# Seven products in place of eight for the gates of two branches, and copies of flipped attention rows on ScalarE, in one decoder layer

## The chip, the cores and the metric

The kernel runs on one core of a Trainium2 chip. The metric is the device time of one execution in microseconds (us). TensorE (PE in the rows) does matmuls into eight PSUM banks; VectorE (DVE), ScalarE (ACT) and GpSimd (POOL) do the element-wise work; SyncE (SP) starts most DMAs. Every engine runs its own queue strictly in order, and semaphores order the engines against each other.

## The reference, cut to what matters

One layer of a decoder for 512 prompt tokens and 8x8 sample tokens, 576 rows in all, all in float32. Three branches (A a conformer convolution, B an attention over the best-scoring keys, C a gated MLP over chunks) are each projected, gated and added:

```python
h = x * (1 + sc1) + sh1
z = jnp.einsum('btd,de->bte', h, w_in) + b_in
a_glu, q, k, v, qi, ki, wi, uv, gate_logits = jnp.split(z, SPLIT_OFFSETS, axis=-1)
...
g_a, g_b, g_c = jnp.split(jax.nn.sigmoid(gate_logits), 3, axis=-1)
merged = g_a * (y_a @ w_pa) + g_b * (y_b @ w_pb) + g_c * (y_c @ w_pc)
x = layer_norm(ALPHA * x + (1 + g1) * (merged @ w_o), ln1_g, ln1_b)
h2 = x * (1 + sc2) + sh2
x = layer_norm(ALPHA * x + (1 + g2) * moe(h2, ...), ln2_g, ln2_b)
```

A gate is a product of h (1024 wide) with a 1024x1024 part of w_in, a projection one of y (512 wide) with a 512x1024 matrix. The attention picks 128 keys for a prompt row (66 for a sample row) by the scores of an indexer, and `moe` routes each row to two of 16 experts.

## The kernel before

A list of steps, `plan`, is written by hand in `make_plan` and `full_plan`, and every engine's block walks the same list and issues its own part of each step; so the list sets the order of all five queues. Activations lie transposed, features on partitions: `HT` holds h as 8 slices of 128 features by 576 tokens, `YT` the branches' outputs as 4 slices. Tokens are worked in two halves of 288 (`HALF`).

The stage at issue has 48 pairs of a gate and a projection, (branch, tile f of 128 output features, half h), first A, then C, then B. `("gate", x, f, h)` is 8 matmuls of 128x128 weights with 128x288 activations into one bank, `("proj", x, f, h)` 4 such matmuls (L1923 in both, a helper). ScalarE takes a tanh of the gate (L1194) and a copy of the projection (L1201), GpSimd adds one to the tanh, multiplies and adds it to `MG` (L912, L917, L918; the last two pairs go to VectorE, L1742 and L1744). `GT` and `PJ`, the outputs of ScalarE, have two buffers each, and `merged` counts finished pairs.

Between the pairs of A and C stand the steps of the attention, by the table `sides`, in units of 128 prompt rows and two heads: `dots` (indexer scores, L2119; VectorE L1613, L1616, L1618), `tk` (top-k rounds of VectorE, L1345 and L1346), `lg` (logits on TensorE, L2152; softmax on VectorE from L1640 to L1655 with exponents on ScalarE, L1062), `pt` (flips of the probabilities through TensorE, L1927, and a copy of the result from PSUM to `PTT` on VectorE, L1668) and `pv` (product with the values, L2193, copied by VectorE, L1682). A unit's `lg`, `pt` and `pv` stand one pair apart. The units grow: 128, 256, 384 and 512 keys. `("pv", "s")` is the last of them, for the sample rows (L2198 and L2203), and VectorE then prepares rows for the layer norm (`prepare_rows`, L1356 to L1360) from transfers that start behind it.

PSUM banks are used in three rings: three banks for gates and projections (`mm`), two for flips (`tt`), three for attention products (`at`). A step waits for the bank to be freed by whoever read it last. Behind the stage come W_o (L1957), layer norm, the router, which sets `order_known`, and the experts, whose weights SyncE brings in behind that.

## Time and profile before

| | |
|---|---|
| runs of the kernel before | 1064.9, 1067.6, 1067.71 us; median 1067.6 |
| profiled execution | 1068.1 us, of it span 1066.0 |
| mean granted clock of TensorE | 0.971 |
| busy over the span | PE 1006.0 us (94%), DVE 497.1 (47%), POOL 248.7 (23%), ACT 188.0 (18%) |
| gates and projections of A, C, B | about 276 to 406, 406 to 540, 540 to 639 us |
| W_o, layer norm, router | 640 to about 740 us |
| experts | about 740 to 1030 us |

A share of busy time is a mean over stages with different limits, so the rows below are read by stretch. A timeline's row gives start, duration (of a run of instructions that follow each other, with their count), engine, line, and in brackets the idle time ahead of it with what ended it. A float32 matmul leaves two records. A duration that stands behind a count covers the whole run; a mean in ns is that of one instruction and overlaps its neighbours on TensorE.

### The profile page before, as it was taken

What the parts mean: (1) busy time and instruction counts of PE and PEld (TensorE: products, weight loads), DVE (VectorE), ACT (ScalarE), POOL (GpSimd) and SP (SyncE); (2) the same over time, 40 slices, a digit from 0 to 9 for tenths busy, and PEclk for the clock granted to TensorE, in tenths of its full rate; (3) what the DMA queues carried; (4) which work ended last, traced back from release to release, by engine and by line L of the source; (5) the groups of instructions that cost most, each with busy time, mean ns of one, the idle gap of its engine ahead of it and who ended that gap; (6) DMA issues with size and microseconds to landing.
All of it is one profiled execution on the core that took longest, in us unless ns stands there. A gap on an engine that the chain in (4) does not pass through costs nothing. (4 is left out here: it accounts for less than half of the span.)

```text
span 1066.0 us, 23313 instructions
## 1 busy us (share of the span) xinstructions
PE 1006.0 (94%) x9543; PEld 705.4 (66%) x9543; DVE 497.1 (47%) x1295; ACT 188.0 (18%) x444; POOL 248.7 (23%) x284
## 2 busy tenths in 40 slices
PE   4999999999999999999999999986998999999994
PEld 3777777567776767667777774565666666866663
DVE  2122899983467888855114003678322221101146
ACT  2010112213221222221111110011111111111104
POOL 0000002734121213222335420000211212422123
PEclk8998999999999999999999999996999999999997
DMA  9964743654505206114072309134599899999994
GB/s 308 308 131 132 219 159 112 219 188 137 208 13 173 65 17 201 45 32 119 11 180 77 119 1 365 40 137 180 221 420 419 340 409 396 414 393 409 408 251 92
DMA packets 94001, 214.96 MB, mean 202 GB/s; under 512 B 23572, under 2 KB 48407, under 8 KB 89797
## 3 DMA queue, kind: packets, MB, share of 16 engines
q1 hardware_dynamic: 78388, 186.20, 49.0%
q0 software_dynamic: 6672, 19.67, 6.1%
q10 hardware_dynamic: 8841, 7.64, 2.6%
q8 instruction: 77, 1.26, 0.5%
q14 instruction: 23, 0.19, 0.1%
HBM read 201.12 MB, written 16.92 MB: 205 GB/s over the span
## 5 line engine op out<-in xcount | busy, mean ns | idle before, releaser
L1923 PE MATMUL banks<-arena 128*128 128x288 f32 (+7 forms) x1842 | 446.9, 398 | 6.0 <-issue 2.1
L1923 PEld LDWEIGHTS banks<-arena 128*128 128x128 f32 (+2 forms) x1842 | 332.1, 192 | 113.1 <-issue 31.3
L2308 PE MATMUL banks<-arena 128*32 128x256 f32 x3136 | 183.4, 382 | 5.8 <-issue 4.5
L2308 PEld LDWEIGHTS banks<-arena 128*32 128x32 f32 x3136 | 113.0, 109 | 66.7 <-issue 8.2
L1851 DVE TENSOR_TENSOR arena<-arena,banks 128x128 f32<-128x128 f32 x49 | 14.1, 288 | 215.0 <-ACT arena L1240 214.7
L2330 PE MATMUL banks<-arena 128*32 128x256 f32 x1568 | 95.3, 378 | 0.0
L912 POOL TENSOR_SCALAR arena<-arena 128x288 f32<-128x288 f32 x46 | 43.1, 937 | 198.8 <-ACT arena L1194 198.8
L970 POOL DMA_INDIRECT expert_rows<-arena,ints x44 | 42.9, 974 | 190.7 <-ACT arena L1251 190.7
L1317 DVE SCALAR_TENSOR_TENSOR arena<-arena 128x512 f32<-128x512 f32 x120 | 82.0, 744 | 0.0
L1937 PE MATMUL banks<-arena 128*128 128x288 f32 x256 | 69.2, 428 | 2.7 <-DVEq L1335 2.7
L2330 PEld LDWEIGHTS banks<-arena 128*32 128x32 f32 x1568 | 53.5, 109 | 23.2 <-issue 0.4
L1937 PEld LDWEIGHTS banks<-arena 128*128 128x128 f32 x256 | 49.9, 199 | 19.2 <-DVEq L1335 4.3
L1957 PE MATMUL banks<-arena 128*128 128x512 f32 x128 | 56.5, 594 | 1.1 <-DVE arena L1744 1.1
L1927 PE MATMUL banks<-arena 128*128 128x128 f32 (+7 forms) x295 | 45.1, 283 | 12.4 <-DMA arena<-constants 4.9
L1927 PEld LDWEIGHTS banks<-arena 128*128 128x128 f32 (+7 forms) x295 | 33.6, 147 | 25.7 <-issue 13.6
L1194 ACT ACTIVATE arena<-banks,arena 128x288 f32<-128x288 f32 x48 | 24.0, 501 | 132.3 <-PE banks L1923 128.9
L1957 PEld LDWEIGHTS banks<-arena 128*128 128x128 f32 x128 | 23.7, 189 | 29.0 <-issue 29.0
L876 POOL TENSOR_TENSOR arena<-arena 9x512 f32<-9x512 f32 x8 | 13.2, 1652 | 126.0 <-ACTq L1089 126.0
L1240 ACT ACTIVATE arena<-banks 128x128 f32<-128x128 f32 x49 | 13.6, 278 | 161.5 <-PE banks L2308 161.5
L858 POOL TENSOR_TENSOR arena<-arena 128x1 f32<-128x1 f32 (+1 forms) x15 | 8.4, 560 | 118.4 <-DVE arena L1298 118.4
L1251 ACT ACTIVATE arena<-banks,arena 128x256 f32<-128x256 f32 x44 | 20.9, 474 | 76.0 <-PE banks L2330 76.0
L917 POOL TENSOR_TENSOR arena<-arena 128x288 f32<-128x288 f32 x30 | 25.6, 854 | 33.7 <-ACT arena L1201 33.4
(303 smaller groups left out, 938.9 us busy)
## 6 DMA issues: line engine op xcount, KB each, us to landing
arena<-in_w_e_gate SPq DMA_DIRECT2D x16, 2048.0 KB, 13.0
arena<-in_w_e_up SPq DMA_DIRECT2D x16, 2048.0 KB, 14.9
arena<-in_w_e_down SPq DMA_DIRECT2D x16, 2048.0 KB, 21.2
arena<-in_w_ada SPq DMA_DIRECT2D x8, 2048.0 KB, 10.6
arena<-in_w_in SPq DMA_DIRECT2D x8, 2048.0 KB, 9.8
arena<-in_w_ada SPq DMA_DIRECT2D x8, 1024.0 KB, 11.6
arena<-in_x_prompt SPq DMA_DIRECT2D x8, 512.0 KB, 6.4
arena<-in_w_in SPq DMA_DIRECT2D x14, 256.0 KB, 8.2
```

The lines of the kernel that those rows point to most:

```text
L912: own.link(pool.tensor_scalar(GT[:, z, :], GT[:, z, :], 1.0, None, ALU.add))
L917: own.link(pool.tensor_tensor(PJ[:, z, :], GT[:, z, :], PJ[:, z, :], ALU.mult))
L970: pool.indirect_dma_start(quarters, bass.IndirectOffsetOnAxis(ints[:, I_DEST + d:I_DEST + d + 1], 0), YR[:, yr_of(d), :], None).then_inc(s ...
L1194: act.activation(GT[:, n % 2, :], mm.tile(key)[:, 0:HALF], ACT.Tanh, bias=PARH[:, r:r + 1], scale=0.5).then_inc(mm.free(key), 1)
L1251: act.activation(YR[:, yr_of(d), :], banks[6 + d % 2][:, 0:256], ACT.Copy, scale=WBLK[:, d:d + 1]).then_inc(ev("yo_up"), 1)
L1317: stt(ACC[:, j, 0:SEQ], arena[:, bass.ds(w + (A_AE + j * EXT), SEQ)], arena[:, bass.ds(w + (A_CK + j * CW), 1)], ACC[:, j, 0:SEQ], ALU.mul ...
L1923: last = pe.matmul(out, a, b, start=k == 0, stop=k == len(pairs_) - 1)
L1927: return pe.transpose(out, src, ident[0:src.shape[0], 0:src.shape[0]])
L1937: return pe.matmul(early_in(key).tile(key)[:, 0:HALF], a_rows[:, k, a:a + P], HT[:, k, h * HALF:h * HALF + HALF], start=k == 0, stop=k == ...
L1957: last = pe.matmul(ps, MG[:, k, t * P:t * P + P], w[k], start=k == 0, stop=k == KT - 1)
L2308: last = pe.matmul(out, HG[:, g % 2, k, a:a + BLK], both_weights(i, k, c), start=k == 0, stop=k == KT - 1)
L2330: last = pe.matmul(banks[6 + b % 2][BLK * c:BLK * c + BLK, 0:256], HETB[:, b % 2, k, :], w[:, k, 256 * c:256 * c + 256], start=k == 0, sto ...
```

## The change

**Gates.** Eight pairs of tiles, f and f+1 with f = 0, 2, 4, 6 of C and of B (`FAST`), are computed together as a 2x2 block product: the weights in quarters w11, w12, w21, w22 (half of the contraction by tile), the activations in quarters x11, x12, x21, x22 (half of the contraction by half of the tokens). Seven products of four matmuls each, step `("seven", x, m, k)`, take the place of four gates of eight: 1 = w11 x11, 2 = w12 x21, 5 = s1 t1, 6 = s2 t2, 3 = s4 x22, 7 = s3 t3, 4 = w22 t4. The sums s of the weights (step `("sum", "w", m, k)`, four of 128x512 for each pair, the third one written over w21) and t of the activations (`("sum", "t", k)`, four of 128x1152, once) are made by VectorE, L1488 in the kernel after. The results are added up by VectorE too, seven additions of 128x288 a pair, in PSUM or into the buffers `part` and `cross`; ScalarE copies product 1 to `part`, and takes the tanh of a product only when VectorE has added to it (`seven_added`).

**Projections.** For the pairs f = 0, 2, 4 of B (`FIVE`) the projections are made in the same way, `("five", ...)`: seven products of two matmuls, four sums of weights of 128x256 (`"v"`) for each pair, four of activations of 128x576 (`"y"`) once, and seven additions a pair. These products use the `at` ring.

**Order.** The sums of the first pair's weights stand behind the attention steps of pair ("A", 7, 0); the sums of activations stand between products 1 and 2 of the first pair of C; other pairs' weight sums stand in the pair ahead. Within a pair of C the order is 1, 2, attention, 6, projection, 5, attention, 3, projection, 7, attention, projection, 4, projection, attention. `prepare_rows` is split into ten steps that stand in the last two pairs of `FIVE`.

**Flipped rows.** The copies of `pt` for the prompt units go from VectorE (L1668) to ScalarE. The copies for the sample rows stay.

**Others.** A few semaphores are merged (the convolution's weights into `small_in`, and three of the router into `routed_full`), 1024 floats are added to the arena, and the scratch for software DMA is set to 8192.

```diff
+A_SUMS = A_SM + 164
+A_END = A_SUMS + 2 * 512
...
+FAST = [("C", f) for f in (0, 2, 4, 6)] + [("B", f) for f in range(0, KT, 2)]
+FIVE = [m for m, (x, f) in enumerate(FAST) if x == "B" and f < KT - 2]
+SUMS_AFTER = {("A", KT - 1, 0): [("sum", "w", 0, k) for k in range(4)]}
...
-    for x in "AC":
-        for f in range(KT):
-            for h in range(2):
-                plan += [("gate", x, f, h), ("proj", x, f, h)] + sides[n]
-                n += 1
-    plan += [("gate", "B", 0, 0), ("pv", "s"), ("gate", "B", 0, 1), ("proj", "B", 0, 0), ("proj", "B", 0, 1)]
-    for f in range(1, KT):
+    for x, f in [("A", f) for f in range(KT)] + [("C", f) for f in range(FAST[0][1])]:
         for h in range(2):
-            plan += [("gate", "B", f, h), ("proj", "B", f, h)]
+            plan += [("gate", x, f, h)] + ([("sum", "t", 2)] if (x, f, h) == ("C", 3, 1) else [])
+            plan += [("proj", x, f, h)] + sides[n] + SUMS_AFTER.get((x, f, h), [])
+            n += 1
+
+    for m, (x, a) in enumerate(FAST):
+        g = lambda *ks: [("seven", x, m, k) for k in ks]
+        proj = lambda f, h: [("proj", x, a + f, h)]
+        nxt = lambda *ks: [("sum", "w", m + 1, k) for k in ks] if m + 1 < len(FAST) else []
+        rows = lambda *ks: [("rows", "ps"[m - FIVE[1]], k) for k in ks] if m in FIVE[1:] else []
+        side = lambda k: sides[16 + 2 * FAST[0][1] + 4 * m + k] if x == "C" else []
+        if m not in FIVE:
+            late = [("sum", "t", k) for k in range(4)] if (m, FAST[0][1]) == (0, 0) else []
+            plan += g(1) + late + g(2) + side(0) + g(6) + proj(0, 0) + g(5) + side(1) + g(3) + nxt(0) + proj(0, 1) + g(7) + nxt(1, 2)
+            plan += side(2) + proj(1, 1) + g(4) + nxt(3) + proj(1, 0) + side(3)
+            continue
+        q = lambda *ks: [("five", x, m, k) for k in ks]
+        own = lambda *ks: [("sum", "v", m, k) for k in ks]
+        y = lambda k: [("sum", "y", k)]
+        if m == FIVE[0]:
+            plan += g(1) + [("pv", "s")] + g(2) + own(0, 1) + g(6) + y(0) + g(5) + y(1) + q(1, 2) + y(2) + own(2) + g(3) + nxt(0)
+            plan += q(6) + y(3) + own(3) + q(5, 3) + nxt(1) + g(7) + nxt(2) + q(7) + nxt(3) + g(4) + q(4)
+            continue
+        plan += g(1) + q(1) + g(2) + q(2) + own(0, 1) + g(6) + rows(0) + q(6) + own(2) + g(5) + rows(1) + q(5) + own(3) + g(3) + nxt(0) + q(3) + nxt(1)
+        plan += g(7) + nxt(2) + q(7) + rows(2) + nxt(3) + g(4) + rows(3) + q(4) + rows(4)
...
+            elif kind == "seven":
+                _, x, m, k = key
+                if k == 1:
+                    act.wait_ge(*mm.full(key))
+                    if m:
+                        act.wait_ge(*added(m - 1, 4))
+                    act.activation(part, mm.tile(key)[:, 0:HALF], ACT.Copy).then_inc(mm.free(key), 1)
+                elif k in tile_of:
+                    x, f, h = fast_tile(m, k)
+                    n = pair_no[(x, f, h)]
+                    act.wait_ge(*added(m, k))
+                    act.wait_ge(ev("merged"), n - 1)
+                    r = R_G + "ABC".index(x) * KT + f
+                    act.activation(GT[:, n % 2, :], mm.tile(key)[:, 0:HALF], ACT.Tanh, bias=PARH[:, r:r + 1], scale=0.5).then_inc(mm.free(key), 1)
...
+            elif kind == "five" and key[3] == 1:
+                m = key[2]
+                act.wait_ge(*at.full(key))
+                if m > FIVE[0]:
+                    act.wait_ge(*added_y(m - 1, 4))
+                act.activation(part_y, at.tile(key)[:, 0:HALF], ACT.Copy).then_inc(at.free(key), 1)
...
+            elif kind == "pt" and key[1] != "s":
+                _, i, c = key
+                u = unit_no[(i, c)]
+                if u == 0:
+                    act.wait_ge(ev("cv_out"), 16 * 9)
+                else:
+                    act.wait_ge(*at.full(("pv",) + units[u - 1]))
+                k = P * (i + 1)
+                for n in range(NKV):
+                    kk = key + (n,)
+                    act.wait_ge(*tt.full(kk))
+                    act.activation(PTT[:, n, 0:k], tt.tile(kk)[:, 0:k], ACT.Copy).then_inc(tt.free(kk), 1)
...
+        def half_sum(key):
+
+            what, m, k = key[1], key[2], key[-1]
+            if what in "ty":
+                x11, x12, x21, x22 = h_quarters if what == "t" else y_quarters
+                t1, t2, t3, t4 = t_sums if what == "t" else y_sums
+                if k == 0:
+                    dve.wait_ge(*(mm.full(("proj", "A", KT - 1, 1)) if what == "t" else mm.full(("proj", "C", KT - 1, 0))))
+                else:
+                    dve.wait_ge(*summed(what, min(k - 1, 1)))
+                if (what, k) == ("t", 2) and FAST[0][1]:
+                    dve.wait_ge(*mm.full(("gate", "C", 3, 1)))
+                out, a, b, op = ((t1, x12, x11), (t2, x22, t1), (t3, x22, x12), (t4, x21, t2))[k] + (ALU.subtract,)
+            else:
+                w11, w12, w21, w22 = w_quarters(m, 4 if what == "w" else 2)
+                s1, s2, s4 = w_sums if what == "w" else v_sums
+                if k == 0:
+                    x, a = fast_pair(m)
+                    dve.wait_ge(*arrived_at[("g", x, a // 4)])
+                    if what == "w" and m:
+                        dve.wait_ge(*mm.full(fast_key("seven", m - 1, 3)))
+                    if what == "v" and m > FIVE[0]:
+                        dve.wait_ge(*at.full(fast_key("five", m - 1, 3)))
+                else:
+                    dve.wait_ge(*summed(what, m, k - 1))
+                out, a, b, op = ((s1, w21, w22, ALU.add), (s2, s1, w11, ALU.subtract), (s4, w12, s2, ALU.subtract), (w21, w11, w21, ALU.subtract))[k]
+            tt_(out, a, b, op).then_inc(ev("summed"), 1)
...
+        def seven(key, ps):
+
+            _, x, m, k = key
+            ps = ps[:, 0:HALF]
+            if k == 2:
+                dve.wait_ge(*mm.taken(fast_key("seven", m, 1)))
+                tt_(ps, ps, part, ALU.add).then_inc(ev("seven_added"), 1)
+            elif k == 6:
+                dve.wait_ge(*added(m, 2))
+                tt_(part, ps, part, ALU.add).then_inc(ev("seven_added"), 1)
+                dve.wait_ge(*added(m, 6))
+                dve.sem_inc(mm.free(key), 1)
+            elif k == 5:
+                tt_(cross, ps, part, ALU.add).then_inc(ev("seven_added"), 1)
+                dve.wait_ge(*added(m, 5))
+                dve.sem_inc(mm.free(key), 1)
+            elif k == 3:
+                tt_(ps, ps, cross, ALU.add).then_inc(ev("seven_added"), 1)
+            elif k == 7:
+                tt_(part, ps, part, ALU.add).then_inc(ev("seven_added"), 1)
+                dve.wait_ge(ev("seven_added"), 7 * m + 5)
+                tt_(ps, ps, cross, ALU.add).then_inc(ev("seven_added"), 1)
+            elif k == 4:
+                dve.wait_ge(*added(m, 7))
+                tt_(ps, ps, part, ALU.add).then_inc(ev("seven_added"), 1)
...
+            dve.wait_ge(*added_y(m, k))
+            dve.sem_inc(at.free(key), 1)
...
-                if key == ("pv", "s"):
-                    prepare_rows()
...
+            elif kind in ("seven", "five"):
+                _, x, m, k = key
+                n, w_, t_ = (4, "w", "t") if kind == "seven" else (2, "v", "y")
+                if k == 1:
+                    got(("g", x, fast_pair(m)[1] // 4))
+                if key == ("five", "B", FIVE[0], 1):
+                    pe.wait_ge(ev("yb_up"), 17)
+                if k in (5, 6, 3, 7):
+                    pe.wait_ge(*summed(w_, m, {5: 0, 6: 1, 3: 2, 7: 3}[k]))
+                if k in (5, 6, 7, 4):
+                    pe.wait_ge(*summed(t_, {5: 0, 6: 1, 7: 2, 4: 3}[k]))
+                w, x_ = fast_operands(m, n)[k]
+                last = group(ps[:, 0:HALF], [(w[:, j, :], x_[:, j, :]) for j in range(n)])
...
-    nc = bacc.Bacc("TRN2", target_bir_lowering=False, num_devices=1)
+    nc = bacc.Bacc("TRN2", target_bir_lowering=False, num_devices=1, dynamic_dma_scratch_size=8192)
```

The queue of VectorE around the start of C, before: the top-k rounds end, then the copy of `pv` (L1682), the copies of `pt` (L1668) and the softmax (L1640 to L1655).

```order
L1345 MAX arena<-arena 128x8
L1346 MATCH_REPLACE arena<-arena 128x512
L1682 COPY arena<-banks 128x128
L1668 COPY arena<-banks 128x384 x2
L1640 SCALAR_TENSOR_TENSOR arena<-banks,arena 128x384
L1649 ISA arena<-arena 128x384
L1649 ISA arena 128x1
L1651 TENSOR_SCALAR arena<-arena 128x1
```

The same queue now, from the end of the rounds in the last step of A: L1488 are the sums of activations, L1496 the addition to product 2, L1880 the copy of `pv`, L1850 the softmax's first instruction.

```order
L1457 MAX arena<-arena 128x8
L1458 MATCH_REPLACE arena<-arena 128x512
L1488 TENSOR_TENSOR arena<-arena 128x1152 x2
L1488 TENSOR_TENSOR arena<-arena 128x4x288
L1488 TENSOR_TENSOR arena<-arena 128x1152
L1496 TENSOR_TENSOR banks<-banks,arena 128x288
L1880 COPY arena<-banks 128x128
L1850 SCALAR_TENSOR_TENSOR arena<-banks,arena 128x384
```

The four sums and an addition now stand between the rounds and the copy of `pv`, and the copies of `pt` are gone. A little further on, behind that softmax, stand the additions to products 6 (L1499) and 5 (L1503), behind three top-k rounds:

```order
L1864 RECIPROCAL arena<-arena 128x1
L1865 TENSOR_SCALAR arena<-arena 128x384
L1457 MAX arena<-arena 128x8
L1458 MATCH_REPLACE arena<-arena 128x512
L1457 MAX arena<-arena 128x8
L1458 MATCH_REPLACE arena<-arena 128x512
L1457 MAX arena<-arena 128x8
L1458 MATCH_REPLACE arena<-arena 128x512
L1499 TENSOR_TENSOR arena<-banks,arena 128x288
L1503 TENSOR_TENSOR arena<-banks,arena 128x288
L1880 COPY arena<-banks 128x128
```

So a bank that product 6 holds is freed only when VectorE has gone through the rounds. TensorE's queue at the start of C before, from the logits (L2152) at the end of A through one gate and its projection to the attention steps that follow (L2193 `pv`, L1927 `pt`):

```order
L2152 MATMUL banks<-arena 128x384 [waits at_free1]
L2152 MATMUL banks<-arena 128x384 [waits at_free2]
L1923 MATMUL banks<-arena 128x288 [waits slot_in3,mm_free2]
L1923 MATMUL banks<-arena 128x288 x7
L1923 MATMUL banks<-arena 128x288 [waits slot_in3,mm_free0]
L1923 MATMUL banks<-arena 128x288 x3
L2193 MATMUL banks<-arena 64x128 [waits t_free0,t_free1,at_free0]
L2193 MATMUL banks<-arena 64x128 x5
```

And now, from the logits of the first attention step within the pair on: product 6, a projection, product 5, the next attention step and product 3 (all products and projections are L2119).

```order
L2350 MATMUL banks<-arena 128x384 [waits at_free2]
L2119 MATMUL banks<-arena 128x288 [waits summed,mm_free2]
L2119 MATMUL banks<-arena 128x288 x3
L2119 MATMUL banks<-arena 128x288 [waits yct_up,slot_in3,mm_free0]
L2119 MATMUL banks<-arena 128x288 x3
L2119 MATMUL banks<-arena 128x288 [waits summed,mm_free1]
L2119 MATMUL banks<-arena 128x288 x3
L2391 MATMUL banks<-arena 64x128 [waits t_free0,t_free1,at_free0]
L2391 MATMUL banks<-arena 64x128 x5
L2123 MATMUL banks<-arena 128x128 [waits probs_ready,t_free1]
```

Gates of eight matmuls that waited for weights and a bank have become products of four, and three of each seven products wait for VectorE's sums (`summed`).

## Rows read from the trace of the kernel before

**Rows 1.** Busy time by stretch: PE, PEld, DVE, ACT, POOL, granted clock, DMA share, GB/s
```profile
380.00:400.00 20.00, 19.24 (x69) 12.33 (x68) 15.71 (x40) 4.92 (x13) 3.49 (x5) 0.91 0.10 26
400.00:420.00 20.00, 19.44 (x111) 13.96 (x110) 16.93 (x46) 5.80 (x14) 6.70 (x13) 1.00 0.68 225
420.00:440.00 20.00, 20.00 (x134) 14.12 (x133) 18.41 (x40) 3.15 (x8) 7.57 (x9) 1.00 0.16 47
...
600.00:620.00 20.00, 20.00 (x84) 15.53 (x83) 0.00 (x0) 3.23 (x7) 7.89 (x10) 1.00 0.09 33
```

**Rows 2.** TensorE's waits, 280 to 660: us in total, times, longest
```profile
PE banks L2152 <- DVE arena L1682: 1.2, 1, 1.2
PE banks L1957 <- DVE arena L1744: 1.1, 1, 1.1
```

**Rows 3.** Timeline of TensorE in A: start, us, then the run
```profile
332.70 0.70 PE L2152 MATMUL banks<-arena 64*128 64x256 f32 x2 [1.22 <-DVE arena L1682]
333.94 0.70 PE L2152 MATMUL banks<-arena 64*128 64x256 f32 x2 [0.54 <-DVE arena L1613]
334.56 7.78 PE L1923 MATMUL banks<-arena 128*128 128x288 f32 x24
...
385.17 1.07 PE L2152 MATMUL banks<-arena 64*128 64x384 f32 x2 [0.60 <-DVE arena L1616]
386.18 7.57 PE L1923 MATMUL banks<-arena 128*128 128x288 f32 x24
```

**Rows 4.** Timeline of TensorE in C and B
```profile
406.43 6.09 PE L1923 MATMUL banks<-arena 128*128 128x288 f32 x24
412.46 0.88 PE L2193 MATMUL banks<-arena 128*64 128x128 f32 x12
...
414.92 6.10 PE L1923 MATMUL banks<-arena 128*128 128x288 f32 x24
...
435.23 1.13 PE L2152 MATMUL banks<-arena 64*128 64x512 f32 x4
...
438.28 6.10 PE L1923 MATMUL banks<-arena 128*128 128x288 f32 x24
...
592.01 46.86 PE L1923 MATMUL banks<-arena 128*128 128x288 f32 x192 [0.30 <-PE banks L1923]
```

**Rows 5.** Timeline of VectorE around the start of C and at the rows' preparation
```profile
403.45 0.68 DVE L1346 MATCH_REPLACE8 arena<-arena 128x512 f32<-128x512 f32 x1
...
406.63 0.56 DVE L1640 SCALAR_TENSOR_TENSOR arena<-banks,arena 128x384 f32<-128x384 f32 x1
...
410.87 0.69 DVE L1345 MAX8 arena<-arena 128x8 f32<-128x512 f32 x1
...
415.42 0.29 DVE L1682 COPY arena<-banks 128x128 f32<-128x128 f32 x1
...
571.75 0.69 DVE L1356 TENSOR_SCALAR arena<-arena 128x1024 f32<-128x1024 f32 x1 [21.92 <-DMA arena<-in_ln_b]
...
575.59 1.82 DVE L1360 TENSOR_TENSOR arena<-arena 128x1024 f32<-128x1024 f32 x1
...
581.75 1.81 DVE L1360 TENSOR_TENSOR arena<-arena 64x1024 f32<-64x1024 f32 x1
```

**Rows 6.** VectorE's groups by line and shape, 280 to 660: busy us, mean ns
```profile
L1668 DVE COPY arena<-banks 128x512 f32<-128x512 f32 x8 | 5.2, 686 | 1.7 <-PE banks L1927 1.7
L1618 DVE TENSOR_TENSOR arena<-arena 128x512 f32<-128x512 f32 x3 | 2.1, 693 | 0.1
L1359 DVE TENSOR_TENSOR arena<-arena 128x1024 f32<-128x1024 f32 x1 | 1.2, 1225 | 0.0
L1742 DVE SCALAR_TENSOR_TENSOR arena<-arena,banks 128x288 f32<-128x288 f32 x2 | 0.9, 454 | 54.4 <-PE banks L1923 54.4
```

**Rows 7.** Busy time by stretch, the experts (columns as in rows 1)
```profile
740.00:1030.00 290.00, 285.04 (x5193) 190.21 (x5189) 63.04 (x179) 41.64 (x105) 68.29 (x71) 0.99 0.93 371
```

**Rows 8.** Timeline of GpSimd in B
```profile
576.41 1.66 POOL L918 TENSOR_TENSOR arena<-arena 128x288 f32<-128x288 f32 x1
...
587.35 0.79 POOL L918 TENSOR_TENSOR arena<-arena 128x288 f32<-128x288 f32 x1
```

More of the change, by code:

```diff
@@ L527, in build_in, with fast_tile @@
     pos = {k: n for n, k in enumerate(plan)}
-    pairs = [(x, f, h) for x in "ACB" for f in range(KT) for h in range(2)]
+    tile_of = {2: (0, 0), 3: (0, 1), 7: (1, 1), 4: (1, 0)}
+    def fast_tile(m, k):
+        x, a = fast_pair(m)
+        return x, a + tile_of[k][0], tile_of[k][1]
+    pairs = [k[1:] if k[0] == "proj" else fast_tile(k[2], k[3]) for k in plan if k[0] == "proj" or k[0] == "five" and k[3] in tile_of]
     pair_no = {k: n for n, k in enumerate(pairs)}
@@ L904, in _ @@
                 rstd(rows_of(key[1]))
-            elif kind == "proj":
-                _, x, f, h = key
+            elif kind == "proj" or kind == "five" and key[3] in tile_of:
+                x, f, h = key[1:] if kind == "proj" else fast_tile(key[2], key[3])
                 n = pair_no[(x, f, h)]
@@ L910, in _ @@
                     continue
-                pool.wait_ge(*mm.taken(("gate", x, f, h)))
+                pool.wait_ge(*gate_up(x, f, h))
                 own.link(pool.tensor_scalar(GT[:, z, :], GT[:, z, :], 1.0, None, ALU.add))
-                pool.wait_ge(*mm.taken(key))
+                pool.wait_ge(*(mm.taken(key) if kind == "proj" else added_y(key[2], key[3])))
                 if x == "A":
@@ L1486, in _ @@
                 continue
+            if kind == "sum":
+                half_sum(key)
+                continue
+            if kind == "rows":
+                prepare_rows(*key[1:])
+                continue
             ring_of = {"M": mm, "T": tt, "A": at}[ring_name(key)]
-            mine = kind in ("par", "ck", "ws", "st", "cT", "mT", "xTs", "bd", "lnA1", "mix", "dots", "wo", "cum", "near")
+            mine = kind in ("seven", "five") and key[3] > 1 or kind in ("par", "ck", "ws", "st", "cT", "mT", "xTs", "bd", "lnA1", "mix", "dots", "wo", "cum", "near")
             if mine:
@@ L1564, in _ @@
                     conv()
+            elif kind == "seven" and key[3] > 1:
+                seven(key, ps)
+            elif kind == "five" and key[3] > 1:
+                five(key, ps)
             elif kind == "lnA1":
@@ L1979, in _ @@
                 continue
+            if kind in ("sum", "rows"):
+                continue
             ring_of = {"M": mm, "T": tt, "A": at}[ring_name(key)]
@@ L2154, in _ @@
                 else:
[L2155 removed]
+                    pe.wait_ge(ev("masked_up"), 2 + c + 1)
                     if c == 0:
```

135 lines of the change are left out of this document (97 added, 38 removed), and 2 rows, old and new, of the table kinds.

## The prediction

> **What bounds the kernel now.** I read four views in this order. The busy time by stretch [rows 1] shows TensorE at 19 to 20 of every 20 us from the gates of A to the end of the gates of B: this stage is bound by matmuls. It also shows what else is full: VectorE is busy 16.93 and 18.41 us of 20 in 400 to 440, where branch C begins, and has nothing to do in 600 to 620. TensorE's waits between 280 and 660 [rows 2] are few; the longest are 1.2 us before logits in A and 1.1 before W_o. The timeline of TensorE [rows 3] shows what the waits in A cost beyond themselves: after 1.22 and 0.54 us the next gate and projection (24 records) took 7.78 us, after 0.60 us they took 7.57, against 6.09 elsewhere [rows 4]. The granted clock of the stretch with the second is 0.91, that of its neighbours 1.00 [rows 1]: part of it ran at the lower level (1.2 of 2.4 GHz). So such a wait costs its length and some 1.5 to 1.7 us behind it. Last, what follows this stage: from 740 to 1030 the DMA share is 0.93 at 371 GB/s [rows 7]. These are expert weights, whose transfers from the third expert on wait for the routing, and the routing for W_o. A microsecond gained before W_o starts that stage a microsecond earlier and isn't taken back by it; I count it in full.
>
> **Matmuls saved.** A gate is 8 and a projection 4 matmuls of 128x288, two records each. In C 24 records start 6.03 us apart (406.43 to 412.46, [rows 4]): 0.5025 us for one matmul, 4.02 for a gate, 2.01 for a projection or one of the seven products. In B 192 records take 46.86 us [rows 4], 0.488 for a matmul. Eight pairs go from 32 to 28 matmuls and three pairs of projections from 16 to 14: 16 fewer in C, 8.0 us, and 22 fewer in B, 10.7 us. Nothing hides matmuls in this stage, so all 18.7 us lie on the path, if what the new products wait for is ready.
>
> **Flipped rows to ScalarE.** VectorE loses 32 copies of up to 0.686 us [rows 6]. ScalarE is busy 3 to 6 us of 20 here [rows 1]; TensorE issues the product that such a copy waits for ahead of its flips, so I see no new wait there. In A this takes VectorE time away right ahead of the waits on logits, 1.22 + 0.54 + 0.60 = 2.4 us. A little may remain, and a few waits on the copies themselves go as well. I take 2.4; the bounds are 0 (the logits wait for something else) and 2.9.
>
> **The first pair of C: the new waits.** This decides the result. I walk VectorE's queue with durations of before, in the clock of before (both engines come some 2.4 us earlier, which moves both alike). VectorE ends the top-k rounds ahead of C at 404.13 [rows 5]. Now come four sums of weights, 128x512; such a sum takes 0.693 [rows 6], 0.72 with the gap: 2.9. Then the copy of an attention product, 0.5 with its semaphore, a unit's softmax, 406.63 to 410.87, 4.24, and three top-k rounds, 410.87 to 415.42, 4.55 [rows 5]: 416.3. Only then stand the sums of the activations, 128x1152. From 0.693 at 512 and 1.225 at 1024 [rows 6] the slope gives 1.36; one sum at 1024 took 1.82 [rows 5], which would make 2.0. I take 1.4, since the 1.82 goes with GpSimd at work (rival 2) and GpSimd has no gate to work on at this point. The second of them is ready at 419.1.
> - Product 6 needs it. TensorE starts C at 406.43, does two products (4.02) and the attention step (412.46 to 414.92, 2.46 [rows 4]) and stands at 412.9: **6.2 us of waiting**.
> - Product 3 needs the bank of product 6, so VectorE's addition of product 6. In the queue before it stand two more sums (2.8), an addition, a copy (0.5), a softmax (4.24) and three rounds (4.55). An addition of 128x288 I price by the nearest row, 0.454 [rows 6], 0.5 with the gap and up to 0.65 where it waits for itself. From 419.1 that makes 432.2. TensorE needs three times 2.01, then 0.9 for one attention product, 426.1, waits for the softmax's rows at 427.1 (**1.0 us**), does 0.9 of flips, and from 428.0 waits for the bank: **4.3 us**.
> - In the second pair the flips of the first 512-wide unit wait for its softmax. From 431.7 VectorE has six additions (3.2), two copies (1.0), seven rounds with their end (11.0), four sums (2.9) and this softmax (4.24 grows by its width to some 5.0): 454.8. TensorE has from 432.3 eight groups of 2.01 and attention steps of 0.9 and 3.05 (435.23 to 438.28, [rows 4]): 452.3, **2.5 us of waiting**.
>
> Small waits of this kind behind it I put at 1.0; VectorE then works its backlog off. The new waits are 6.2 + 1.0 + 4.3 + 2.5 + 1.0 = 15.0 us. Branch C becomes 15.0 - 8.0 = **7.0 us longer**, not shorter.
>
> **Branch B.** A pair with both kinds of products is 42 matmuls, 20.5 us of TensorE. VectorE has 14 additions (7.0 to 9.1), four sums of 512 (2.9), four of 256 (0.43 each by the slope, 1.7) and, in two pairs, half of the rows' preparation (ten instructions from 571.75 on [rows 5] to 583.6, so 5.9): 17.5 to 19.6 of 20.5. The rows arrive at 571.75 and were waited for [rows 5]; their first use now comes one pair behind the last attention product, about 4 us after they are there. So B waits for nothing and keeps its 10.7 us. The wait before W_o stays, 1.1 [rows 2].
>
> **Other edits.** The merged semaphores let the first flips also wait for the convolution's weights, which are on their way before w_ada that TensorE waits for next: nothing, with a bound of 1 us. The smaller scratch for software DMA I put at nothing (rival 4).
>
> **The sum:** -2.4 (A) + 7.0 (C) - 10.7 (B) = **-6.1 us**. Clock: the two slow stretches in A may go (-1.5 and -1.7), and the waits of product 6, product 3 and the flips are long enough to bring new ones; the first of those is taken up by the wait behind it, two remain, +3.2. I let them cancel. The profiled execution took 1068.1 (span 1066.0 and 2.1 around it), 0.5 over the median: 1068.1 - 6.1 = **1062.0**.
>
> **Rivals.**
> 1. *The clock takes the rest.* The waits in A stay with their slow stretches (0 in place of -2.4), and two or three new slow stretches of 1.6 follow in C: -6.1 + 2.4 + 3.2 to 4.8 gives 1067.6 to 1069.2; half of that, 1065. For: the waits of [rows 3] were each followed by one. Against: just those waits hang on VectorE's queue, which is shortened right there. In a sentence apart: the Trainium skill, TensorE: Matmul & The Clock Gate, Part 1, says that the engine is throttled by default and activity releases it; the trace agrees with its 0.91.
> 2. *Slower: the sums and GpSimd stand in each other's way.* VectorE's product of two 128x1024 SBUF operands took 1.82 at 575.59 [rows 5] and 1.225 one instruction earlier [rows 6]; beside the long one GpSimd's took 1.66, later 0.79 [rows 8]. If every half sum is stretched by that 0.59, product 6 comes 6 x 0.59 = 3.5 us later and product 3 another 1.2; in B eight sums add 4.7, and with additions at 0.65 VectorE has 24.3 against 20.5, 3.8 in two pairs and nothing in the one without rows: 7.6. Together 12.3: 1062.0 + 12.3 = **1074**. It turns from faster to slower at a mean stretch of 0.59 x 6.1 / 12.3 = 0.29 us. Against: GpSimd works 7.89 of 20 us in B [rows 1], so a good half of the sums meet nothing, and the 512-wide sums of before show no stretch. The Trainium skill, SBUF — State Buffer, section Who interferes with whom, speaks against this change here: a VectorE instruction with two SBUF inputs and a GpSimd one that reads SBUF lock each other out for a whole instruction. The trace agrees in that both grew.
> 3. *The sums are covered.* If VectorE has the activations' sums early enough, all 18.7 us remain with A's 2.4: **1047**. For: the count of matmuls is certain. Against: 16.93 and 18.41 of 20 us [rows 1]; the queue is in order, and the sums stand behind 12 us of other work.
> 4. *The scratch.* GpSimd issues 67 indirect transfers; if half of the room makes it wait for earlier ones, some ten that the routing and the last experts wait for cost 1 us each: 1072. GpSimd is busy 68.29 of 290 us there [rows 7], so it has room.
>
> **How the numbers follow.** Forecast 0.58, its own range 1057 (shortest prices, -1.8, and A's clock won, -3.2) to 1066 (activation sums at 2.0 and additions at 0.65, +4). Rival 1: 0.20. Rival 2: 0.09. Rival 3: 0.09. Rival 4: 0.03; others 0.01. The range 1055 to 1069 takes in the forecast and most of rival 1 and leaves out 2 in 10. A measurement of this kernel can tell about 0.3%, 3.2 us. Faster, under 1064.4: nine tenths of the forecast, a quarter of rival 1, and rival 3: 0.66, I say 0.68. Within 0.3%: 0.20. Slower: rivals 2 and 4: 0.12.
>
> **What would show it.** Right: TensorE's waits have a product behind VectorE's sums with some 6 us and one behind an addition with some 4 us, both in 405 to 435; branch C is longer by 5 to 9 us, B shorter by 11; the waits on logits at 332 and 385 are gone. Wrong: no wait over 2 us in the first pair (rival 3), slow stretches over more than two gates (rival 1), TensorE waiting for additions in 560 to 630 and half sums well over 0.7 us (rival 2), or GpSimd waiting behind 740 (rival 4).

## The result, and the profile after

The changed kernel takes 1056.5 us (median of five runs, 1055.63 to 1059.77) against 1066.0 before (median of five, 1064.90 to 1067.71). The ratio on record is 0.9901 with a 95% interval of 0.9876 to 0.9925. (It is not the quotient of the two medians, which is 0.9911; the ratios further down differ from the quotients of their medians by up to 0.3%, too.) The forecast was 1062.0 with a range of 1055 to 1069 and "faster" at 0.68. The sign is right and the time lies in the range, though just under the 1057 to 1066 that the forecast gave for itself, without the rivals; the gain of the profiled execution, 1066.0 - 1055.5 = 10.5 us of span, is larger than the 6.1 I had summed, and the way it is put together is what the rest is about.

Where it came from is read from TensorE's timeline, as the time between the first products of A, of C, of B, and of W_o:

| | A starts | A | C | B | behind W_o's start |
|---|---|---|---|---|---|
| before | 275.98 | 130.45 | 133.67 | 99.91 | 426.0 |
| after | 275.66 | 123.71 | 140.00 | 89.93 | 426.2 |
| difference | -0.3 | **-6.7** | **+6.3** | **-10.0** | +0.2 |

The first products of A, B and W_o in TensorE's timeline of the kernel before (that of C is in [rows 4]):

```profile
275.98 6.09 PE L1923 MATMUL banks<-arena 128*128 128x288 f32 x24
...
540.10 4.05 PE L1923 MATMUL banks<-arena 128*128 128x288 f32 x16
...
640.01 20.88 PE L1957 MATMUL banks<-arena 128*128 128x512 f32 x48 [1.14 <-DVE arena L1744]
```

C, in which 16 matmuls were saved, became longer; A, in which none was, became shorter by nearly the same. TensorE's timeline of the kernel after (compare [rows 3, 4]; the starts of A, C, B and W_o are its first row and those at 399.37, 539.37 and 629.30):

```profile
275.66 6.10 PE L2119 MATMUL banks<-arena 128*128 128x288 f32 x24
...
331.26 1.47 PE L2350 MATMUL banks<-arena 64*128 64x256 f32 x4
332.66 6.09 PE L2119 MATMUL banks<-arena 128*128 128x288 f32 x24
...
379.75 0.91 PE L2350 MATMUL banks<-arena 64*128 64x384 f32 x2 [0.29 <-DVE arena L1826]
380.59 6.09 PE L2119 MATMUL banks<-arena 128*128 128x288 f32 x24
...
399.37 4.15 PE L2119 MATMUL banks<-arena 128*128 128x288 f32 x16
...
412.48 8.21 PE L2119 MATMUL banks<-arena 128*128 128x288 f32 x24 [5.86 <-DVE arena L1488]
...
425.17 6.10 PE L2119 MATMUL banks<-arena 128*128 128x288 f32 x24 [2.85 <-DVEq L1501]
...
446.99 0.63 PE L2123 MATMUL banks<-arena 128*128 128x128 f32 x4 [1.76 <-DVE arena L1865]
...
539.37 2.11 PE L2119 MATMUL banks<-arena 128*128 128x288 f32 x8
...
629.30 20.88 PE L2153 MATMUL banks<-arena 128*128 128x512 f32 x48 [1.15 <-DVE arena L1940]
```

The logits in A (L2350) no longer wait for more than 0.29 us, and the two runs of 24 records behind them take 6.09 us where they took 7.78 and 7.57 [rows 3]. C starts at 399.37 in place of 406.43. Then come the new waits: product 6 for the sums of activations (5.86), product 3 for the bank that VectorE frees (2.85), the flips of the first 512-wide unit for its softmax (1.76). The list of TensorE's waits between 270 and 660 (us in total, times, longest; compare [rows 2]) has the same three at its head; behind them stands the wait ahead of W_o, unchanged (1.15, the last row above):

```profile
PE banks L2119 <- DVE arena L1488: 5.9, 1, 5.9
PE banks L2119 <- DVEq L1501: 2.9, 1, 2.9
PE banks L2123 <- DVE arena L1865: 2.7, 4, 1.8
```

VectorE's timeline tells why, and is the walk of the prediction in real numbers (compare [rows 5]):

```profile
396.75 0.68 DVE L1458 MATCH_REPLACE8 arena<-arena 128x512 f32<-128x512 f32 x1
397.47 2.88 DVE L1488 TENSOR_TENSOR arena<-arena 128x512 f32<-128x512 f32 x4
...
409.58 5.42 DVE L1488 TENSOR_TENSOR arena<-arena 128x1152 f32<-128x1152 f32 x4
414.91 0.46 DVE L1496 TENSOR_TENSOR banks<-banks,arena 128x288 f32<-128x288 f32 x1
...
424.60 0.46 DVE L1499 TENSOR_TENSOR arena<-banks,arena 128x288 f32<-128x288 f32 x1
```

Between the weights' sums and the activations' stand 9 us of softmax and top-k rounds, and between the addition to product 2 (L1496) and that to product 6 (L1499), which frees the bank, another 9 us. TensorE is idle meanwhile; by stretch (columns as in [rows 1]):

```profile
400.00:410.00 10.00, 6.21 (x37) 3.98 (x35) 8.76 (x24) 1.83 (x5) 0.00 (x0) 1.00 0.77 255
410.00:420.00 10.00, 7.52 (x22) 5.65 (x23) 8.89 (x18) 3.02 (x8) 0.93 (x1) 0.66 0.16 45
...
600.00:620.00 20.00, 20.00 (x84) 15.52 (x83) 11.93 (x19) 3.32 (x7) 13.10 (x13) 1.00 0.00 1
```

In 400 to 410 TensorE is busy 6.21 of 10 us and VectorE 8.76; in 410 to 420 the granted clock is 0.66, part of the stretch at the lower level, right behind the wait of 5.86. In B VectorE and GpSimd have much more to do than before (11.93 and 13.10 of 20 us, against 0.00 and 7.89 [rows 1]), and TensorE is busy all the time.

### The profile page after: what moved, and what is told of

Same layout as the page of the kernel before. It is cut to its first block and busy times, and to the rows that moved or that the text cites. A ratio compares the mean times of both kernels' runs of the same rounds, so it can differ in the third digit from the quotient of the medians.

```text
span 1055.5 us, 23403 instructions
## 1 busy us (share of the span) xinstructions
PE 987.6 (94%) x9467; PEld 687.0 (65%) x9467; DVE 554.7 (53%) x1392; ACT 199.0 (19%) x475; POOL 256.2 (24%) x284
## 5 line engine op out<-in xcount | busy, mean ns | idle before, releaser
L2119 PE MATMUL banks<-arena 128*128 128x288 f32 (+6 forms) x1766 | 427.9, 397 | 15.2 <-DVE arena L1488 5.9
L2119 PEld LDWEIGHTS banks<-arena 128*128 128x128 f32 (+1 forms) x1766 | 317.0, 192 | 118.3 <-issue 38.3
L2519 PEld LDWEIGHTS banks<-arena 128*32 128x32 f32 x3136 | 110.3, 110 | 70.6 <-issue 9.6
L2541 PEld LDWEIGHTS banks<-arena 128*32 128x32 f32 x1568 | 52.0, 109 | 23.7
L1488 DVE TENSOR_TENSOR arena<-arena 128x512 f32<-128x512 f32 (+3 forms) x52 | 40.4, 781 | 2.9 <-DVE arena L1526 0.6
L997 POOL TENSOR_TENSOR arena<-arena 128x288 f32<-128x288 f32 x30 | 29.2, 972 | 48.4 <-ACT arena L1281 40.7
L1295 ACT ACTIVATE arena<-banks,arena 128x288 f32<-128x288 f32 x32 | 16.0, 501 | 112.4 <-DVE banks L1507 40.7
## 6 DMA issues: line engine op xcount, KB each, us to landing
arena<-in_w_e_up SPq DMA_DIRECT2D x16, 2048.0 KB, 15.1
```

The costliest lines, as they stand in the source:

```text
L997: own.link(pool.tensor_tensor(PJ[:, z, :], GT[:, z, :], PJ[:, z, :], ALU.mult))
L1295: act.activation(GT[:, n % 2, :], mm.tile(key)[:, 0:HALF], ACT.Tanh, bias=PARH[:, r:r + 1], scale=0.5).then_inc(mm.free(key), 1)
L1488: tt_(out, a, b, op).then_inc(ev("summed"), 1)
L2119: last = pe.matmul(out, a, b, start=k == 0, stop=k == len(pairs_) - 1)
L2519: last = pe.matmul(out, HG[:, g % 2, k, a:a + BLK], both_weights(i, k, c), start=k == 0, stop=k == KT - 1)
L2541: last = pe.matmul(banks[6 + b % 2][BLK * c:BLK * c + BLK, 0:256], HETB[:, b % 2, k, :], w[:, k, 256 * c:256 * c + 256], start=k == 0, sto ...
```

## The experiments

Theory Q, as the prediction had it: VectorE's in-order queue decides. What frees it in A (the flips on ScalarE) is a gain; what is put into it at C's start costs more than the matmuls saved there. Rival M: the gain is the saved matmuls, and A became shorter by something else in the change. The stage lengths of the profiles, read as above. The part behind W_o's start lasts from 420.5 to 428.1 us and differs by 1.5 and 2.8 us between two profiles of one kernel, so the stages tell more than the totals. Two versions had one run each, and two kernels were run a second time:

| kernel | A | C | B | behind | median us | before beside it | ratio, 95% interval |
|---|---|---|---|---|---|---|---|
| flips only | 123.70 | 133.42 | 99.92 | 428.0 | 1059.4 | 1067.9 | 0.9949 (0.9926 to 0.9973) |
| after, flips back | 128.78 | 149.39 | 89.94 | 428.1 | 1064.4 | 1067.9 | 0.9955 (0.9927 to 0.9982) |
| after, C as before | 123.70 | 133.42 | 89.92 | 423.7 | 1047.4 | 1067.9 | 0.9827 (0.9794 to 0.9859) |
| after, C's first two pairs as before | 123.69 | 129.67 | 89.94 | 423.9 | 1041.6 | 1067.9 | 0.9762 (0.9742 to 0.9783) |
| after, C's first pair as before | 123.73 | 138.76 | 89.92 | 424.2 | 1051.1 | 1069.2 | 0.9823 (0.9771 to 0.9876) |
| after, sums early | 123.74 | 143.41 | 89.94 | 427.3 | one run, 1062.5 | 1069.2 | |
| after, wait filled | 123.73 | 141.73 | 89.94 | 420.5 | one run, 1053.5 | 1069.2 | |
| before, smaller scratch | 130.22 | 133.63 | 99.92 | 421.6 | 1064.3 | 1069.2 | 0.9971 (0.9947 to 0.9994) |
| after, once more | 123.73 | 143.03 | 89.95 | 427.7 | 1057.4 | 1068.7 | 0.9883 (0.9829 to 0.9937) |
| after, C's first two pairs as before, once more | 123.72 | 129.66 | 89.95 | 426.7 | 1041.9 | 1068.7 | 0.9751 (0.9706 to 0.9797) |

**Flips only.** The kernel before with the copies of flipped prompt rows on ScalarE (the waits around the copies move with them):

```diff
...
-                        dve.tensor_copy(PTT[:, n, 0:k], tt.tile(kk)[:, 0:k]).then_inc(tt.free(kk), 1)
...
+                    act.activation(PTT[:, n, 0:k], tt.tile(kk)[:, 0:k], ACT.Copy).then_inc(tt.free(kk), 1)
```

> The kernel before with one part of the change: ScalarE copies the flipped rows. Medians so far: before 1066.0, after 1056.5. Theory Q (VectorE's in-order queue decides: freeing it removes the waits on logits at 332 and 385 and the two slow stretches behind them, 3.5 + 3.2 us): about 1059, A 6.7 us shorter, C and B as before. Rival M (the gain of the change is its saved matmuls, and A became shorter by something else in the change, the merged semaphores or the smaller scratch): 1064 to 1066.

Measured: 1059.4, and A is 123.70 us, the very length of the kernel after; B is that of before, and C 0.25 us shorter. The two places in A, in TensorE's timeline of this kernel:

```profile
327.11 1.47 PE L2152 MATMUL banks<-arena 64*128 64x256 f32 x4
328.51 6.09 PE L1923 MATMUL banks<-arena 128*128 128x288 f32 x24
...
375.60 0.91 PE L2152 MATMUL banks<-arena 64*128 64x384 f32 x2 [0.29 <-DVE arena L1628]
376.44 6.09 PE L1923 MATMUL banks<-arena 128*128 128x288 f32 x24
```

No wait over 0.29 us is left, and no slow stretch. So the whole gain in A is this edit, and rival M, which put it down to something else in the change, falls.

**Flips back.** The kernel after with that edit reversed.

> The kernel after with the flipped rows copied by VectorE again. Theory Q: the 6.7 us in A come back with both slow stretches, and the first pair of C waits 1 to 3 us longer, since the copies stand in the same queue as the sums: 1064 to 1066, so that the saved matmuls alone bring next to nothing. Rival M: 1057 to 1059.

Measured: 1064.4, from 1058.9 to 1074.6; by the ratio, the saved products alone are worth 0.45%. (Line numbers of VectorE are lower by 12 here than in the kernel after: L1476 is L1488 there.) A has the waits again (1.20 and 0.54 us, then 24 records in 7.78; then 0.60), but behind the 0.60 no slow stretch followed, where both were expected to come back; so A is 5.1 us longer than in the kernel after and not 6.7. C is 9.4 us longer, where 1 to 3 was expected. Its waits grew by 0.8 us in all; its clock fell three times, as TensorE's timeline shows:

```profile
386.54 6.10 PE L2119 MATMUL banks<-arena 128*128 128x288 f32 x24
...
419.07 8.75 PE L2119 MATMUL banks<-arena 128*128 128x288 f32 x24 [5.85 <-DVE arena L1476]
...
432.66 8.79 PE L2119 MATMUL banks<-arena 128*128 128x288 f32 x24 [3.23 <-DVEq L1489]
...
457.89 0.63 PE L2123 MATMUL banks<-arena 128*128 128x128 f32 x4 [0.35 <-DVE arena L1853]
458.45 1.95 PE L2350 MATMUL banks<-arena 64*128 64x512 f32 x4
460.32 3.64 PE L2328 MATMUL banks<-arena 64*32 64x256 f32 x32
...
464.10 8.44 PE L2119 MATMUL banks<-arena 128*128 128x288 f32 x24
```

Two stretches of 24 records take 8.75 and 8.79 us, where the kernel after had 8.21 and 6.10, and from 458 to 472, behind waits of 1.50 and 0.35, everything is slow (1.95 for logits that take 1.13, 3.64 for 1.94). This profile is the slowest of the ten runs of this kernel, so 149.4 is an upper end.

**C as before.** The kernel after with eight matmuls for all gates of C; B keeps its seven and five products, and the activations' sums come in the middle of C:

```diff
-FAST = [("C", f) for f in (0, 2, 4, 6)] + [("B", f) for f in range(0, KT, 2)]
-SUMS_AFTER = {("A", KT - 1, 0): [("sum", "w", 0, k) for k in range(4)]}
+FAST = [("B", f) for f in range(0, KT, 2)]
+SUMS_AFTER = {("C", 4, 0): [("sum", "t", k) for k in (0, 1, 3)], ("C", KT - 1, 0): [("sum", "w", 0, k) for k in range(4)]}
...
```

> The kernel after with all gates of C as before (eight matmuls each, 16 matmuls more, 8.0 us); the activations' sums stand in C where VectorE has room, B keeps its seven and five products. Theory Q: C's 14 us of waits go and cost more than the 8.0 us of matmuls: C about 133.7 us as before, total about 1050. Rival M: 1056.5 + 8.0 = 1064.5.

Measured: 1047.4, C 133.42 us. Doing 16 matmuls more makes C 6.6 us shorter than in the kernel after, as theory Q has it and against rival M's 1064.5.

**C's first two pairs as before.** The same for f = 0 and 2 only; the sums stand where VectorE has worked off the attention:

```diff
+FAST = [("C", f) for f in (4, 6)] + [("B", f) for f in range(0, KT, 2)]
+SUMS_AFTER = {("C", 2, 1): [("sum", "t", k) for k in (0, 1, 3)], ("C", 3, 0): [("sum", "w", 0, k) for k in range(4)]}
...
```

> The kernel after with the first two pairs of C as before and seven products only from the tile pairs 4 and 6 of C on (8 matmuls more than after, 4.0 us); the activations' sums come where VectorE has worked off the attention's backlog. Theory Q: no wait over 1 us in C, C 4.0 us shorter than before, 10 us shorter than after: about 1046; up to 1049 if the rows for B's preparation, whose transfers start behind the last attention product, are then waited for. Rival M: 1060.5.

Measured: 1041.6, the best of all. C is 129.67: 4.0 us below before, and 3.75 below the version above, which has the same flips on ScalarE and all gates of C with eight matmuls. Eight matmuls are 4.02 at 0.5025, so the products cost 0.3 us beside them. TensorE has no wait of note between A and W_o but the one ahead of W_o that the kernel before has too; the others are 0.4 us or less each:

```profile
PE banks L2153 <- DVE arena L1940: 1.1, 1, 1.1
```

VectorE is not idle here: it is busy 9.15 of 10 us in 470 to 480. But its sums end at 473.2, and the first product that needs one, product 6, starts at 482.11. TensorE's first products of C and of B, product 6, and the sums on VectorE:

```profile
400.31 6.10 PE L2119 MATMUL banks<-arena 128*128 128x288 f32 x24
...
468.99 4.25 DVE L1488 TENSOR_TENSOR arena<-arena 128x512 f32<-128x512 f32 x5
...
482.11 6.10 PE L2119 MATMUL banks<-arena 128*128 128x288 f32 x24
...
529.98 2.11 PE L2119 MATMUL banks<-arena 128*128 128x288 f32 x8
```

So the products cost next to nothing beyond their matmuls when VectorE has the sums ready in time. The stages are 20.7 us shorter than before (6.8 + 4.0 + 10.0), as expected. The median is 26 below that of its neighbour. The profiled execution, 22.2 us of span below that of before, is the slowest of the five, and no faster one was profiled, so where the rest lies is not shown. It may lie in the parts ahead of A and behind W_o, which differ from profile to profile (A starts between 271.5 and 276.6, and behind W_o's start come 420.5 to 428.1 us).

Once more, beside the kernel after on another occasion:

> The version with two plain pairs of C once more. Theory Q: stages as in its first profile (A 123.7, C 129.7, B 89.9 us), 0.976 to 0.980 of before, 11 to 14 us below the kernel after on the same chip, and less scatter, since no long wait is left that the clock could answer.

> The kernel after once more, beside the version with two plain pairs of C on the same chip. Theory Q and the rival C (the clock only adds scatter): 0.99 of before; C 140 us or more, since the slow stretch behind the waits differs from run to run, and A 123.7 as in every kernel whose flips ScalarE copies.

Measured: 1041.9 (0.9751, where 0.976 to 0.980 was expected) and 1057.4 (0.9883), 15.5 us apart, somewhat more than the 11 to 14 expected. The stages repeat: A 123.72 and 123.73, B 89.95 and 89.95, and C 129.66 for the one and 143.03 for the other, against 140.00 in its first profile. Less scatter was expected and isn't seen: 1040.0 to 1047.3 and 1051.2 to 1060.5. In the second profile of the kernel after, C has two slow stretches that the first doesn't have, behind the wait of product 3 and behind the flips:

```profile
423.70 7.78 PE L2119 MATMUL banks<-arena 128*128 128x288 f32 x24 [3.57 <-DVEq L1501]
...
448.87 2.08 PE L2350 MATMUL banks<-arena 64*128 64x512 f32 x4
```

The first is 7.78 us where it was 6.10, the second 1.6 us in all (2.08 for logits that took 1.13, and parts of the rows beside them). Product 6's records, on the other hand, took 7.50 where they had taken 8.21, and product 3 waited 3.57 where it had waited 2.85: the two together are 11.07 and 11.06. From the first product of C, product 3 starts after 25.81 us here and after 25.80 in the first profile. VectorE's queue sets that point, whatever TensorE's clock does ahead of it.

**C's first pair as before.** Seven products in C from f = 2 on, the sums one pair of tiles earlier than above:

```diff
+FAST = [("C", f) for f in (2, 4, 6)] + [("B", f) for f in range(0, KT, 2)]
+SUMS_AFTER = {("C", 1, 0): [("sum", "t", k) for k in (0, 1, 3)], ("C", 1, 1): [("sum", "w", 0, k) for k in range(4)]}
...
```

> The kernel after with only the first pair of C as before; three pairs of C with seven products, their sums among the last attention steps that VectorE is still behind with (4 matmuls fewer than the version with two pairs, 2.0 us). Theory Q: the flips of the first 512-wide unit wait about 4 us for VectorE, more than the 2.0 us saved: C about 132 us, 2 longer than with two pairs (129.7), 8 shorter than after; in all some 2 us above the version with two pairs. Rival L: C 127.7, 2 us below it.

Measured: 1051.1, C 138.76 in place of 132. The wait came as expected, 4.59 us; what was not expected stands behind it, in TensorE's timeline:

```profile
440.34 2.06 PE L2123 MATMUL banks<-arena 128*128 128x128 f32 x8 [4.59 <-DVE arena L1865]
442.33 2.08 PE L2350 MATMUL banks<-arena 64*128 64x512 f32 x4
...
448.12 8.69 PE L2119 MATMUL banks<-arena 128*128 128x288 f32 x24
```

and in the busy time by stretch, where the granted clock (third number from the end) is

```profile
440.00:450.00 10.00, 9.66 (x56) 5.12 (x57) 8.72 (x22) 3.96 (x10) 0.93 (x1) 0.50 0.22 59
450.00:460.00 10.00, 10.00 (x53) 6.82 (x56) 2.11 (x5) 1.50 (x3) 1.59 (x2) 0.83 0.13 48
```

0.50 for a whole stretch. From the flips to the next but one gate this kernel takes 461.83 - 440.34 = 21.5 us; the kernel before takes 15.1 for the same steps. So 6.3 us lie in the clock, more than in the wait itself, and with them the 132 expected become 138.8; rival L's 127.7 is far off.

**Sums early.** The kernel after with the four sums of activations right behind A's last projection:

```diff
+            early = [("sum", "t", k) for k in range(4)] if (x, f, h) == ("A", KT - 1, 1) else []
+            plan += [("proj", x, f, h)] + early + sides[n] + SUMS_AFTER.get((x, f, h), [])
...
-            late = [("sum", "t", k) for k in range(4)] if (m, FAST[0][1]) == (0, 0) else []
+            late = []
```

> The kernel after with the four sums of activations moved ahead in VectorE's queue, to right behind the last projection of A, ahead of the attention steps there. Theory Q (VectorE's queue as a whole is too long at C's start, not one sum too late): product 6 waits no more, but the attention product and the flips ahead of it wait 2.7 and 2.6 us, later waits stay (about 4 for the bank): C's length, from its first product to B's first, stays at 139 to 140 us. Rival L (only the place of the sums is wrong): the 5.9 us go and C is 134 to 135.

Measured: C 143.41. Rival L falls: product 6 waits no more, but its wait is found again two steps ahead and the later one stays, in TensorE's timeline (all lines are one higher in number: L2120 is L2119 of the kernel after):

```profile
406.64 0.88 PE L2392 MATMUL banks<-arena 128*64 128x128 f32 x12 [2.40 <-DVE arena L1881]
410.43 1.74 PE L2124 MATMUL banks<-arena 128*128 128x128 f32 x6 [2.91 <-DVE arena L1866]
...
413.69 7.35 PE L2120 MATMUL banks<-arena 128*128 128x288 f32 x24
...
425.89 7.78 PE L2120 MATMUL banks<-arena 128*128 128x288 f32 x24 [3.24 <-DVEq L1502]
```

2.40 and 2.91 in place of 5.86, then 3.24 for the bank: product 3 starts 25.81 us behind C's first product, as in both profiles of the kernel after. So the slow stretch of 7.35 lies inside the wait for VectorE. The 3.4 us by which C is longer than in the first of these profiles, and which theory Q didn't expect, are the 7.78 and one more slow stretch behind 450; the second of them has the same two, and 143.03.

**Wait filled.** The kernel after with ten more matmuls ahead of product 6:

```diff
+                if (kind, m, k) == ("seven", 0, 6):
+                    for _ in range(10):
+                        pe.matmul(ps[:, 0:HALF], fast_operands(m, n)[2][0][:, 0, :], HT[:, 7, 0:HALF], start=True, stop=True)
```

> The kernel after; TensorE fills its wait ahead of product 6 in the first pair of C with ten more matmuls of 128x288 (5.0 us) whose results product 6 writes over. In the kernel after the 24 records behind the wait of 5.86 us took 8.21 us at a lower clock, and then 2.85 us were spent waiting for product 6's bank. Theory Q: the records take 6.1, and the wait for the bank grows by the 2.1 us won, to about 5, since VectorE's queue sets it: branch C stays at 140 us. Rival C (the slow stretch is on the path): C gets 2 us shorter, 138.

Measured, in TensorE's timeline (L2418 are the added matmuls):

```profile
406.59 5.12 PE L2418 MATMUL banks<-arena 128*128 128x288 f32 x20
412.51 6.08 PE L2119 MATMUL banks<-arena 128*128 128x288 f32 x24 [0.80 <-DVE arena L1488]
...
425.21 8.45 PE L2119 MATMUL banks<-arena 128*128 128x288 f32 x24 [4.37 <-DVEq L1501]
```

With the wait filled, the 24 records behind it run at full speed (6.08, where the two profiles without the filling have 8.21 and 7.50): as far as one profile of it can show, the lower clock there is an answer to the idle time. What was won is spent at the next wait, 4.37 in place of 2.85, and product 3 starts 25.82 us behind C's first product, as without the filling: VectorE's queue sets that point, as theory Q says. But now the clock falls behind this longer wait (8.45 for 6.10), and C is 141.7, so neither number was met.

**Smaller scratch.** The kernel before with one argument more:

```diff
-    nc = bacc.Bacc("TRN2", target_bir_lowering=False, num_devices=1)
+    nc = bacc.Bacc("TRN2", target_bir_lowering=False, num_devices=1, dynamic_dma_scratch_size=8192)
```

> The kernel before with the smaller scratch for software DMA (8192) and nothing else. Theory Q: no change, 1066 to 1068, GpSimd's 67 indirect transfers wait for nothing new. Rival S: GpSimd has to wait for room, some us more, over 1070, and the gain of the change would have been larger without it.

Measured: 1064.3, 0.9971 of the kernel before; rival S falls, the smaller scratch costs nothing that can be seen. All stages are those of before. The interval, 0.9947 to 0.9994, lies just below one, and the part behind W_o was 421.6 us in the profile; since that part differs by more than this from profile to profile, a gain is not shown. It is not excluded either, and every version of the kernel after has the smaller scratch.

## Why the prediction was right, and where not

**Matmuls saved: right, and a little dear.** Two pairs alone give 3.75 us in C for eight matmuls where 0.5025 us each makes 4.02, and B 10.0 us for 22 where I had 10.7. Of the 0.7 missing in B, 0.40 is one gap ahead of a product in B that the profile gives to no releaser; the rest I can't place.

**Flips to ScalarE: the mechanism was right, the term was mis-sized.** -2.4 was forecast and -6.7 came, all of it by this edit alone. Of the 6.7, 3.6 are waits (1.6 at 332, 1.7 at 385, and 0.3 of a flip that waited in 367) and 3.2 are the two slow stretches. For the waits I had counted the three on logits alone, 2.4 with a bound of 2.9. The 3.2 I had in view and let cancel against two new slow stretches in C, one behind the wait of product 3 and one behind the flips. That is the step that failed: in this profile neither came, the 24 records behind product 3's wait took 6.10 us and those behind the flips 6.11. But in the second profile of the same kernel both came, 1.7 and 1.6 us, very nearly the 3.2 that I had priced. So the term can't be forecast from this case as one number, and that the first profile was without it is chance.

**The first pair of C: right.** The walk of VectorE's queue gave waits of 6.2, 1.0, 4.3 and 2.5 us; they are 5.86, 0.35, 2.85 and 2.11 (1.76 + 0.35). The sums of 128x1152 took 1.36 us each, the slope's value. Product 3 waits less than I had, since product 6 ahead of it ran slow (8.21 for 6.1): this first slow stretch lies inside the wait for VectorE, as the prediction had it. C was to become 7.0 us longer and became 6.3. The waits and the slow stretch are 13.3 us of the 14.3 that C has beyond its saved matmuls; 1.0 I can't place.

**B: right.** No wait for additions or sums anywhere in it, in any of the kernels with seven products there (89.92 to 89.95 us).

**The sum.** Forecast -2.4 + 7.0 - 10.7 = -6.1; measured -6.7 + 6.3 - 10.0 = -10.4 in the first profile, and -6.7 + 9.4 - 10.0 = -7.3 in the second. Of the difference in the first, 3.2 is the clock in A, 1.2 its waits, 0.7 C, and 0.7 the other way in B. Behind W_o nothing was taken back in these two profiles (+0.2), as [rows 7] had it, as far as a part that differs by several us from profile to profile can tell.

**The rivals.** *The clock takes the rest* did not come as a whole, since A's waits went; but its new slow stretches in C came in the second profile (3.3 us), and other versions paid more (6.3 us with C's first pair as before). *The sums and GpSimd stand in each other's way* is in the trace, at under half of its turning point. VectorE's groups by shape, 280 to 660 (busy us, mean ns; compare [rows 6]):

```profile
L1488 DVE TENSOR_TENSOR arena<-arena 128x512 f32<-128x512 f32 x32 | 25.8, 806 | 1.0 <-DVE arena L1535 0.5 <-DVE arena L1538 0.2
L1488 DVE TENSOR_TENSOR arena<-arena 128x1152 f32<-128x1152 f32 x4 | 5.3, 1358 | 0.1
L1499 DVE TENSOR_TENSOR arena<-banks,arena 128x288 f32<-128x288 f32 x8 | 3.6, 454 | 1.9 <-PE banks L2119 1.8
```

and GpSimd's product in the same view, whose mean before was 0.854 us:

```profile
L997 POOL TENSOR_TENSOR arena<-arena 128x288 f32<-128x288 f32 x30 | 29.2, 972 | 48.4 <-ACT arena L1281 40.7 <-DVE arena L1526 4.3 <-DVE arena L1535 2.1
```

The 512-wide sums take 0.806 us against 0.693 for such a sum before, a mean stretch of 0.11 us where 0.29 would have turned the result (22 of the 32 took 0.68 to 0.72, the other ten 0.85 to 1.34); those of 1152, which run while GpSimd has no gate, show none, and an addition that reads PSUM takes 0.454, as priced. The rule that I had weighed here (the Trainium skill, SBUF — State Buffer, Who interferes with whom) speaks of two instructions that overlap in time; the trace agrees in that both sides grow, and in that 22 of the 32 sums show no stretch. *The sums are covered* was wrong for this kernel, and right for the one that starts them two pairs later. *The scratch* did not come either (1064.3, above).

## What to carry to other kernels

A product that saves matmuls by sums on another engine is worth its matmuls only where that engine has the sums ready in time: here four pairs in C made it 6.3 us longer, and the last two of them alone made it 3.75 us shorter. Look at the queue that must deliver the operands by stretch, not over the span, and walk it instruction by instruction with measured durations; that walk was good to about 1.5 us a wait here. And where two edits come together, do each alone: the copies moved to an engine with room brought 6.7 of the 10.4 us in the stages, more than the arithmetic in the title. (By the ratios of whole runs the two alone are worth about as much, 0.51% and 0.45%.)

## What the runs showed of the hardware that I had not expected

A wait of TensorE has a second price, and it isn't a fixed one. Behind idle times of 2.85 to 5.9 us in C the same 24 records took 6.1 us (behind 2.85), 7.5 and 8.2 (behind 5.85 and 5.86 in two profiles of the same kernel), 7.78 (3.24, 3.57), 8.45 (4.37) and 8.8 (3.23, 5.85); behind 0.60 in A they took 7.57 in the kernel before and 6.10 with the flips back on VectorE; and behind 4.59 the clock stood at 0.50 for a stretch of 10 us and cost 6.3 us in all. Two profiles of the same kernel differ by 3.0 us in C through this, 140.0 and 143.0. What decides between them is left open. Not every slow stretch costs its length: where the next step waits for VectorE all the same, as product 3 does, it costs nothing. The experiment with the filled wait shows, in its one profile, that the lower clock follows from the idle time. The Trainium skill, TensorE: Matmul & The Clock Gate, Part 1, has the lower clock as the state of an idle engine, which activity lifts; the trace agrees in that every slow stretch named here stands behind a wait.
